# A two-block network on one core: the gates of the short layers read from the accumulator bank, one norm for both token tiles, the heads spread over other column steps

## The reference, cut to what matters

```python
for layer in range(2):
    h = _rmsnorm(x, norm_g[layer])
    parts = jnp.split(h @ w_in[layer], 8, axis=-1)
    if layer % 2 == 0:
        qa, ka, va, ga, qb, kb, vb, gb = parts
        oa = _dilated_mixture(rope(qa), rope(ka), va)
        ob = _moba(rope(qb), rope(kb), vb)
    else:
        qc, kc, vc, gc, qd, kd, vd, gd = parts
        oc = _diff_attention(rope(qc), rope(kc), vc, lam, subln_g, lambda_init)
        od = _stick_breaking(qd, kd, vd)
    y = concat([oa * silu(ga), ob * silu(gb)])     # (oc, gc), (od, gd) in the second
    x = x + y @ w_out[layer]
```

## Time and profile before

| | |
|---|---|
| three runs | 2966.28, 2959.11, 2965.33 us; median 2965.33 |
| the profiled execution | 2962.29 us, its span 2960.5 us, so 1.8 us lie around the span |
| mean granted TensorE clock | 0.983 |
| busy: PE, PEld, DVE, ACT, POOL | 96%, 79%, 54%, 47%, 8% |
| the chain that ended last | PE 82%, DVE 8%, ACT 6%, issue 1%, POOL 1%, DMA 1% |

### The profile page before, as it was taken

How to read it: one execution, slowest core, us unless ns; L and a number is a source line. 1 busy time by engine, 2 the same in 40 slices (tenths; PEclk the granted TensorE clock), 3 DMA queues, 4 the chain that set the end, 5 groups by cost and what they waited for, 6 DMA issues and landing times.

```text
span 2960.5 us, 33218 instructions
## 1 busy us (share of the span) xinstructions
PE 2841.2 (96%) x13558; PEld 2346.8 (79%) x13558; DVE 1613.4 (54%) x2004; ACT 1402.6 (47%) x2045; POOL 234.6 (8%) x209
## 2 busy tenths in 40 slices
PE   8899999999999999999999999999999999999986
PEld 6787887777888888888888877788888888877765
DVE  5664666756554554444645545655455444476655
ACT  6554345546444444344544444644444434465563
POOL 0112332300000000000100101000000000011112
PEclk9999999999999999999999999999999999999998
DMA  6654543656666666555664423666666655554422
GB/s 211 123 115 120 106 106 85 122 180 192 185 192 191 185 191 191 187 191 190 192 190 138 140 95 129 191 185 192 191 185 190 191 188 191 190 182 143 135 93 99
DMA packets 212776, 480.85 MB, mean 162 GB/s; under 512 B 15248, under 2 KB 16272, under 8 KB 211984
## 3 DMA queue, kind: packets, MB, share of 16 engines
q1 hardware_dynamic: 210272, 467.57, 54.4%
q0 software_dynamic: 2352, 11.17, 1.1%
HBM read 476.58 MB, written 2.10 MB: 162 GB/s over the span
## 4 chain that ended last, share of the span: by engine, by line
PE 82%; DVE 8%; ACT 6%; issue 1%; POOL 1%; DMA 1%; SPq 0%; DVEq 0%; ACTq 0%; POOLq 0%
PE PS L1013 17%; PE PS L1015 17%; PE PS L1014 17%; PE PS L1062 7%; PE PS L1061 7%; PE PS L1060 7%; DVE WL L1998 2%; ACT WH L1531 1%; DVE WORK L2139 1%; PE PS L1171 1%; DVE XL L1998 1%; PE PS L1270 1%; PE PS L1359 1%; PE PS L1259 1%; PE PS L1086 1%
## 5 line engine op out<-in xcount | busy, mean ns | idle before, releaser
L1998 DVE TENSOR_TENSOR WL<-RAW,WH 128x1024 fp32r<-128x1024 f32 x827 | 1028.4, 1246 | 943.3 <-ACT WH L1531 942.3
L1531 ACT ACTIVATE WH<-RAW 128x1024 fp32r<-128x1024 f32 x831 | 874.5, 1054 | 849.3 <-PE PS L1015 524.0
L1013 PE MATMUL PS<-WH,UTH 128*128 128x512 f32 x2396 | 965.5, 403 | 25.0 <-DVE WL L1998 22.4
L1015 PE MATMUL PS<-WH,UTL 128*128 128x512 f32 x2396 | 939.9, 392 | 0.0
L1014 PE MATMUL PS<-WL,UTH 128*128 128x512 f32 x2396 | 939.3, 392 | 0.0
L1013 PEld LDWEIGHTS PS<-WH,UTH 128*128 128x128 f32 x2396 | 454.0, 189 | 124.7 <-DVE WL L1998 26.3
L1015 PEld LDWEIGHTS PS<-WH,UTL 128*128 128x128 f32 x2396 | 453.2, 189 | 98.4
L1014 PEld LDWEIGHTS PS<-WL,UTH 128*128 128x128 f32 x2396 | 454.4, 190 | 89.9 <-issue 1.9
L1062 PE MATMUL PS<-WH,HTL 128*128 128x512 f32 x656 | 259.3, 395 | 0.0
L1061 PE MATMUL PS<-WL,HTH 128*128 128x512 f32 x656 | 258.8, 394 | 0.0
L1060 PE MATMUL PS<-WH,HTH 128*128 128x512 f32 x656 | 255.4, 389 | 0.0
(11 more groups left out here) (424 smaller groups left out, 2612.2 us busy)
## 6 DMA issues: line engine op xcount, KB each, us to landing
RAW<-in_ffn_w_gu SPq DMA_DIRECT2D x352, 512.0 KB, 4.2
RAW<-in_ffn_w_down SPq DMA_DIRECT2D x176, 512.0 KB, 4.4
RAW<-in_ab_w_in SPq DMA_DIRECT2D x128, 512.0 KB, 4.7
RAW<-in_nsa_w_in SPq DMA_DIRECT2D x80, 512.0 KB, 3.7
RAW<-in_w_in SPq DMA_DIRECT2D x64, 512.0 KB, 3.9
RAW<-in_ab_w_out SPq DMA_DIRECT2D x32, 512.0 KB, 4.4
RAW<-in_nsa_w_out SPq DMA_DIRECT2D x32, 512.0 KB, 3.8
RAW<-in_w_out SPq DMA_DIRECT2D x16, 512.0 KB, 3.8
```

Source lines behind the costliest of these rows:

```text
L1013: e.matmul(o, lh, wh[:, j], start=k + j == 0, stop=False)
L1015: x = e.matmul(o, ll, wh[:, j], start=False, stop=k + j == NKT - 1)
L1531: e.activation(wh, raw, ACTF.Copy).then_inc(*a_hi.inc(s))
L1998: e.tensor_tensor(wl, raw, wh.bitcast(F32), ALU.subtract).then_inc(*v_lo.inc(s))
```

## The change

Steps of the list: `plain` pauses one round more before `pl_s`; `diff` pauses 1 + 2h rounds where it paused h, and its `df_a` is split in two (`df_a`: ScalarE scales row 0, VectorE makes the small factor; `df_b`, a round later: VectorE's sum). `stick` puts `st_z` of heads 0 and 1 in one round, 2 and 3 in the next, and all four `st_l` in one round. `y2d` is one step for both token tiles; `ot 4 0` comes one round later, `ot 5 0` four rounds behind `y2d`. The list of stage 5 becomes: `feat 5 0` R34, `df_s` R35, 37, 39, 41, `df_a` R37, 39, 41, 43, `df_b` R38, 40, 42, 44, `df_t` R39, 41, 43, 45, `st_z` R40, 40, 41, 41, `st_l` R43 (all), `st_m` R44 (all), `st_a` R46, 46, 47, 47, `st_w` R47, 47, 48, 48, `gate2 5 1` R47, `y2d` R49, `ot 5 0` R53; `gate2 5 3`, `st_o` and `ot 5 2` stay in R55, R56, R57.

Operations: for chunks 1 and 3 `z2` copies only the values (128x256); the gate half stays in the bank until `gate2` takes it with one ScalarE Silu into Z2, and that Silu frees the bank. `y2` (stage 4) and the last branch move to VectorE; `st_o` multiplies by the gate as it leaves its bank. GpSimd keeps only the gain times gate of the difference branch.

```diff
-def operand(st, k, *made):
+def operand(st, k, *made, behind=None):
...
-    yield from pause(1 if k in LEFT[st][-4:] else 2)
+    yield from pause(behind or (1 if k in LEFT[st][-4:] else 2))
...
 def plain(br, par, i):
...
-    yield from pause(2 * par + i)
+    yield from pause(1 + 2 * par + i)
...
-def close(st, br, chunk, *parts):
+def close(st, chunk, *parts):
...
-    for i in range(2):
-        yield from need(*parts[i])
-        put("y2", st, br, i)
+    for i, made in enumerate(parts):
+        yield from need(*made)
+        put("y2", st, chunk // 2, i)
...
 def diff(h, i):
...
-    yield from pause(h)
+    yield from pause(1 + 2 * h)
...
+    yield
+    put("df_b", h, i)
...
 def close_diff():
-    yield from need(("z2", 5, 1, 1))
-    put("gate2", 5, 1)
+    yield from need(*[("df_o", h, i) for h in range(4) for i in range(2)])
+    put("y2d")
...
-    for i in range(2):
-        yield from need(*[("df_o", h, i) for h in range(4)])
-        put("y2d", i)
-        yield
...
 def stick(h):
...
-    yield from pause(h)
+    yield from pause(h // 2)
...
-    yield
+    yield from pause(3 - h // 2)
...
-    yield from pause(2)
+    yield from pause(2 + h // 2)
...
-      *[close(4, br, 2 * br + 1, *[[("pl_o", br, par, i) for par in range(2)] for i in range(2)])
+      *[close(4, 2 * br + 1, *[[("pl_o", br, par, i) for par in range(2)] for i in range(2)])
...
-      *[operand(4, k, *[("y2", 4, k // 2, i) for i in range(2)]) for k in (0, 2)])
+      *[operand(4, k, *[("y2", 4, k // 2, i) for i in range(2)], behind=2 - k // 2) for k in (0, 2)])
...
-      close_diff(), close(5, 1, 3, *[[("st_o", h) for h in range(4)]] * 2),
-      operand(5, 0, ("y2d", 0), ("y2d", 1)), operand(5, 2, ("y2", 5, 1, 0), ("y2", 5, 1, 1)))
+      close(5, 1), close_diff(), close(5, 3),
+      operand(5, 0, ("y2d",), behind=4), operand(5, 2, *[("st_o", h) for h in range(4)]))
...
     def gate2_of(chunk, i):
-        base = 2048 + 256 * (i + chunk - 1)
-        return Z2[:, i, 512 * chunk + 256:512 * chunk + 512], WORK[:, base:base + 256]
+        return Z2[:, i, 512 * chunk + 256:512 * chunk + 512]
...
+        elif st == 4:
+            on.wait_ge(*v_b2.of("y", st, k // 2, t))
...
-            on.wait_ge(*g_b2.of("y", st, k // 2, t))
+            on.wait_ge(*(v_b2.of("st_o", 3) if k else v_b2.of("yg")))
...
 def z2(st, part, t):
-    sink(Z2[:, t, 512 * part:512 * part + 512], st, PARTS2.index(part), t, ("z2", st, part, t))
+    c = PARTS2.index(part)
+    if part in (0, 2):
+        sink(Z2[:, t, 512 * part:512 * part + 512], st, c, t, ("z2", st, part, t))
+        return
+    on.wait_ge(*p_mm.of(col_end[st, c]))
+    e.activation(Z2[:, t, 512 * part:512 * part + 256], banks.ap("acc", st, c, t)[:, 0:256], ACTF.Copy,
+                 scale=HR[:, t:t + 1]).then_inc(*a_z.inc("z2", st, part, t))
...
 def gate2(st, chunk):
+    c = PARTS2.index(chunk)
...
-        g, ee = gate2_of(chunk, i)
-        on.wait_ge(*a_z.of("z2", st, chunk, i))
-        e.activation(ee, g, ACTF.Exp, scale=-1.0).then_inc(*a_b2.inc("gate", st, chunk, i))
+        e.activation(gate2_of(chunk, i), banks.ap("acc", st, c, i)[:, 256:512], ACTF.Silu,
+                     scale=HR[:, i:i + 1]).then_inc(*banks.empty(a_b2, "acc", st, c, i))
+        a_b2.also("gate", st, chunk, i)
...
+def df_a(h, i):
+    P, T, s, nk = diff_of(h, i)
+    on.wait_ge(*v_b2.of("df_r", h, i))
+    e.activation(P[:, 0], P[:, 0], ACTF.Copy, scale=s[:, 4:5]).then_inc(*a_b2.inc("df_0", h, i))
...
-def y2d(i):
-    rstd(4, "y2d", i)
+def y2d():
+    on.wait_ge(*a_b2.of("df_o", 3, 1))
+    e.activation(v3(ROT[:, 256:768], 2), Y2[:, :, 0:256], ACTF.Square).then_inc(*a_b2.inc("sq"))
+    rstd(8, "y2d")
...
-def st_o(h):
-    on.wait_ge(*p_b2.of("st_o", h))
-    e.activation(Y2[:, :, 256 + 64 * h:320 + 64 * h], v3(banks.ap("st_o", h)[:, 0:128], 2),
-                 ACTF.Copy).then_inc(*banks.empty(a_b2, "st_o", h))
...
-def gate2(st, chunk):
-    for i in range(2):
-        g, ee = gate2_of(chunk, i)
-        on.wait_ge(*a_b2.of("gate", st, chunk, i))
-        e.tensor_scalar(ee, ee, 1.0, None, ALU.add).then_inc(*v_b2.inc("gate1", st, chunk, i))
-        on.wait_ge(*v_b2.last())
-        e.reciprocal(ee, ee).then_inc(*v_b2.inc("gate", st, chunk, i))
+def y2(st, br, i):
+    y = Y2[:, i, 256 * br:256 * br + 256]
+    on.wait_ge(*a_b2.of("gate", st, 2 * br + 1, i))
+    on.wait_ge(*v_b2.of("pl_o", br, 1, i))
+    e.tensor_tensor(y, y, gate2_of(2 * br + 1, i), ALU.mult).then_inc(*v_b2.inc("y", st, br, i))
...
+def st_o(h):
+    c = 1536 + 256 + 64 * h
+    on.wait_ge(*a_b2.of("gate", 5, 3, 1))
+    on.wait_ge(*p_b2.of("st_o", h))
+    e.tensor_tensor(Y2[:, :, 256 + 64 * h:320 + 64 * h], v3(banks.ap("st_o", h)[:, 0:128], 2),
+                    Z2[:, :, c:c + 64], ALU.mult).then_inc(*banks.empty(v_b2, "st_o", h))
...
-    e.tensor_scalar(P[:, 0], P[:, 0], s[:, 4:5], None, ALU.mult).then_inc(*v_b2.inc("df_0", h, i))
-    on.wait_ge(*v_b2.last())
...
+def df_b(h, i):
+    P, T, s, nk = diff_of(h, i)
+    on.wait_ge(*a_b2.of("df_0", h, i))
+    on.wait_ge(*v_b2.of("df_c", h, i))
...
-def y2d(i):
-    y = v3(Y2[:, i, 0:256], 4)
-    sq = v3(ROT[:, 256 + 256 * i:512 + 256 * i], 4)
-    ss = ST2[:, 64 + 4 * i:68 + 4 * i]
-    on.wait_ge(*g_b2.of("sq", i))
-    e.tensor_reduce(ss, sq, AX, ALU.add).then_inc(*v_b2.inc("ss", i))
+def y2d():
+    y = Y2[:, :, 0:256]
+    ss = ST2[:, 64:72]
+    on.wait_ge(*a_b2.of("sq"))
+    e.tensor_reduce(ss, v3(ROT[:, 256:768], 8), AX, ALU.add).then_inc(*v_b2.inc("ss"))
...
-    rstd(ss, ss, 64, 1.0 - LAMBDA, "y2d", i)
+    rstd(ss, ss, 64, 1.0 - LAMBDA, "y2d")
...
-    e.tensor_tensor(y, y, bc(ss, 64), ALU.mult).then_inc(*v_b2.inc("yn", i))
+    for i in range(2):
+        yi = v3(Y2[:, i, 0:256], 4)
+        e.tensor_tensor(yi, yi, bc(ss[:, 4 * i:4 * i + 4], 64), ALU.mult).then_inc(*v_b2.inc("yn", i))
+    on.wait_ge(*v_b2.last())
+    on.wait_ge(*g_b2.of("gate"))
+    e.tensor_tensor(y, y, Z2[:, :, 768:1024], ALU.mult).then_inc(*v_b2.inc("yg"))
...
 def gate2(st, chunk):
-    for i in range(2):
-        g, ee = gate2_of(chunk, i)
-        on.wait_ge(*v_b2.of("gate", st, chunk, i))
-        e.tensor_tensor(ee, ee, g, ALU.mult).then_inc(*g_b2.inc("gate", st, chunk, i))
...
-def y2(st, br, i):
-    y = Y2[:, i, 256 * br:256 * br + 256]
-    on.wait_ge(*g_b2.of("gate", st, 2 * br + 1, i))
-    on.wait_ge(*(v_b2.of("pl_o", br, 1, i) if st == 4 else a_b2.of("st_o", 3)))
-    e.tensor_tensor(y, y, gate2_of(2 * br + 1, i)[1], ALU.mult).then_inc(*g_b2.inc("y", st, br, i))
...
-def y2d(i):
-    y = v3(Y2[:, i, 0:256], 4)
-    sq = v3(ROT[:, 256 + 256 * i:512 + 256 * i], 4)
-    on.wait_ge(*a_b2.of("df_o", 3, i))
-    e.tensor_tensor(sq, y, y, ALU.mult).then_inc(*g_b2.inc("sq", i))
-    on.wait_ge(*v_b2.of("yn", i))
-    e.tensor_tensor(y, y, rep(SLN, 4), ALU.mult).then_inc(*g_b2.inc("yg", i))
-    on.wait_ge(*g_b2.of("yg", i))
-    on.wait_ge(*g_b2.of("gate", 5, 1, i))
-    e.tensor_tensor(Y2[:, i, 0:256], Y2[:, i, 0:256], gate2_of(1, i)[1], ALU.mult).then_inc(*g_b2.inc("y", 5, 0, i))
+    if (st, chunk) == (5, 1):
+        for i in range(2):
+            g = v3(gate2_of(chunk, i), 4)
+            on.wait_ge(*a_b2.of("gate", st, chunk, i))
+            e.tensor_tensor(g, g, rep(SLN, 4), ALU.mult).then_inc(*g_b2.inc("gate", i))
+        g_b2.also("gate")
...
```

More of the change, by code:

```diff
@@ L1925, in df_t @@
             @step
+            def df_a(h, i):
+                P, T, s, nk = diff_of(h, i)
+                on.wait_ge(*v_b2.of("df_r", h, i))
+                e.activation(P[:, 0], P[:, 0], ACTF.Copy, scale=s[:, 4:5]).then_inc(*a_b2.inc("df_0", h, i))
+            @step
             def df_t(h, i):
@@ L1960, in st_a @@
                 e.activation(L, Zs, ACTF.Exp).then_inc(*a_b2.inc("st_x", h))
-            @step
-            def st_o(h):
-                on.wait_ge(*p_b2.of("st_o", h))
-                e.activation(Y2[:, :, 256 + 64 * h:320 + 64 * h], v3(banks.ap("st_o", h)[:, 0:128], 2),
-                             ACTF.Copy).then_inc(*banks.empty(a_b2, "st_o", h))
             @step
```

2 lines of the change are left out of this document (removed).

## The result

The changed kernel takes 2935.14 us (median of 4 runs, 2933.53 to 2935.63) where the kernel before took 2962.3 beside it. The ratio is 0.9909 [0.9897, 0.9922]. The profiled executions are 2935.07 against 2962.29, their spans 2933.3 against 2960.5: 27.2 us to account for.

What follows compares the result with a forecast made beforehand. PE, busy 96% of the span, was taken as the bound, with its idle time and slow clock to win. 1.8 + 1.7 + 3.1 + 13.7 + 1.9 + 2.8 = 25.0 us off 2962.3 gave 2937.3, stated as 2938; range 2924 to 2952.

Steps and rivals of the forecast that it cites:

- the likeliest case: Whole kernel: the forecast itself, 25.0 us gained, 2938 us; chance 0.50.
- (a): Stage 4 scores a round later: two stops of 0.9 us covered, 1.8 us gained; what moves along taken at zero.
- (c): Middle of stage 5: 12.7 us idle against 20.5, plus 5.9 of clock, 13.7 us gained; bounds 7.8 and 27.
- (b): Last operand of stage 4: Silu and VectorE product end its stop, 1.7 us net, plus 3.1 from the clock.
- (d): Last operand of stage 5: 1.9 us gained despite a 1.4 us bank wait, plus 2.8 from the clock.
- the walk: Middle of stage 5: the step list followed with estimated durations, giving stops of 2.6, 2.6, 4.0, 2.5 and 1.0 us.
- The clock wins nothing: Whole kernel: remaining stops of 1.4 to 4 us keep the clock low; gain 13 us, 2949; chance 0.22.
- The spread covers all: Middle of stage 5: preparations two slots ahead soak up the stops; total gain 38 us, 2924; chance 0.15.
- Rivals 3 and 4: Stage 5: moved df_b stops PE at every df_t; slower, 2977 (chance 0.05), or no change, 2962 (chance 0.08).
- The signs: Stages 4 and 5: no GpSimd stops before line 1077, full clock behind last operands, 1.4 us bank wait, one Ln load.
- one sign of being wrong: Windows behind the stops that remain show clock 0.5 again; the sum then lies at rival 1 or above.
- rival 1: The rival "The clock wins nothing": gain 13 us, 2949 us; chance 0.22.

Runs made afterwards that it cites:

- The undo: The whole change, but stage 4's score softmaxes back in their old round: 2935.45 us, ratio 0.99.
- The kernel with the load taken away: The whole change plus a one-number Silu behind stage 5's norm, so the Silu table loads in idle time: 2931.56 us, ratio 0.9892.
- both spreads are undone: The whole change, but stage 5's difference softmaxes in consecutive rounds and stick-breaking heads one per round: 2939.81 us; with df_b also in df_a's round, 2942.91 us.
- the one with the operations alone: All new operations in the kernel before's old order of steps, stage-4 operands included: 2942.43 us, ratio 0.9921.
- the one with the order alone: The kernel before with only the new pauses of plain, diff and stick, old operations and operand places: 2951.57 us, ratio 0.9955.
- the version with the preparation first: The whole change plus the one-number Silu, and the next slot's preparation ahead of every rope step: 2926.99 us, ratio 0.9871.

## Why the prediction was right, and which of its terms were not

The forecast was 2938 (2937.3 against the profiled execution, which gave 2935.07), by the likeliest case. Its mechanism stands, two of its terms don't, and they fell on opposite sides: stretch by stretch it was 2.2 us too high in (a), 5.2 too low in (c) and 0.8 too high in (b) and (d) together, 25.0 forecast for 27.2 measured. That the sum came out within 2.2 us is in part luck.

**(a) failed.** It took the move of the score softmaxes as two covered stops of 0.9 and "everything behind `pl_s` moves with it" at nothing. The two stops are gone, but the one for the slot behind the second rope, 1.78 before, which I had not looked at, is 2.79, and half of 3.4 us at half clock stands behind it. 1.8 - 1.0 - 1.7 = -0.9, where 1.8 was forecast; PE began stage 4's first stop 0.3 earlier, for a reason ahead of the change, so the table shows -0.4. The undo shows the exchange of stops both ways, and why: PE goes on with that slot 29.4 to 29.6 us behind the first feature transposes in every kernel that keeps the slot behind the rope, whether the scores come a round later or not, so what PE saves ahead of it, it waits there. The 1.7 of clock is not as clear. All eight kernels with the stop of 2.8 have it, but so has the undo, with 1.78.

**(b) held.** 1.9 us measured, 1.7 forecast, and 2.6 from the clock up to the features against 3.1. The 1.41 behind the operand stayed and did not bring the clock down.

**(c) was too small by 5.2 us, and only in the stops.** The two halves of its sum can be taken apart by the window: PE is busy 82.26 of 90.02, so 7.8 idle where I walked to 12.7. Busy time fell by 88.36 - 82.26 = 6.1, where 5.9 was forecast for the clock. The walk's stops against the measured: 2.6 and 1.12 at the first head's `df_b`, 2.6 and 1.94 at the first `st_z`, 4.0 and 2.04 at the third head's `df_b`, 2.5 and 1.69 at the last head's, 1.0 and 0.67 for the slot behind the norm. The places are right, the sizes were walked 1.3 to 2.3 times too large. What made the difference can be seen at the first one (ScalarE's rows, then VectorE's):

```profile
2817.24 0.50 ACT L1928 ACTIVATE WORK<-WORK,SM 128x256 f32<-128x256 f32 x1
...
2817.74 1.99 ACT L1530 ACTIVATE WH<-RAW 128x1024 fp32r<-128x1024 f32 x2
```

```profile
2819.96 0.74 DVE L2454 SCALAR_TENSOR_TENSOR WORK<-WORK,SM 128x128 f32<-128x128 f32 x2
```

Counted from the end of the feature transposes (2802.11 here, 2806.25 in the walk), the second head's exps end at 15.7 us instead of 16.5, and from there to `df_b` there are one copy and one rest as walked. PE goes on at 18.2 instead of 19.2, for the first of the two short `df_b` is enough; and PE came there at 17.1 instead of 16.7. So the chain was walked 0.9 us too long and PE 0.5 us too early, which makes the 1.4 us between 2.5 and 1.12. The other four stops I have not taken apart in this way. On the two spreads the prediction had no separate price, and the runs say that a price for each alone would have misled: their gains don't add.

The norm needed 2878.73 + 0.69 - 2874.66 = 4.8 us from the last `df_o` copy to the gate product, 5 forecast from the earlier trace rows:

```profile
2875.36 0.69 DVE L2462 TENSOR_REDUCE SM<-BIG 128x8 f32<-128x512 f32 x1 [1.77 <-ACT BIG L1951]
...
2877.93 0.76 DVE L2468 TENSOR_TENSOR BIG<-BIG,SM 128x256 f32<-128x256 f32 x2
2878.73 0.69 DVE L2471 TENSOR_TENSOR BIG<-BIG 128x512 f32<-128x512 f32 x1
```

Of the table loads of ScalarE that the prediction counts in the middle, eight became three, as it says. In both stages together 14 became 10, for stage 4 has a new one ahead of its Silu of chunk 1 (2708.21 us, L1914). The ones of the stick-breaking heads are now one for Ln (L1968) and one for the exp behind it (L1974), where the earlier trace rows had four and three.

**(d) held.** 1.7 against 1.9, and the rest of the span 2.5 against 2.8 of clock. The 1.9 had been taken with 1.2 us for the bank's wait, though the working beside it gives 1.4; with that it is 1.7. The bank's stop is 1.36, forecast 1.4, made as the prediction put it (ScalarE):

```profile
2892.33 0.84 ACT L1626 ACTIVATE BIG<-PS,SM 128x256 f32<-128x256 f32 x2 [1.60 <-PE PS L1012]
2893.19 1.28 ACT L1914 ACT_TABLE_LOAD   x1
2894.48 0.84 ACT L1914 ACTIVATE BIG<-PS,SM 128x256 f32<-128x256 f32 x2
```

The load starts 0.02 us behind the copies and the Silu 0.01 behind the load: 1.31 us from the last copy to the Silu, no drain. The Trainium skill, page ScalarE: Activation LUTs, section What ACT_TABLE_LOAD costs, adds a drain of about 1380 ns to each switch. This trace disagrees, and the measurement decides: with the page's drain the stop would have been 1.36 + 1.38 = 2.7 us (an estimate from that page's figure). The kernel with the load taken away lost the whole 1.36.

**The rivals.** "The clock wins nothing" fell: 10.8 us of busy time went. "The spread covers all" fell as well: five stops of 0.7 to 2.0 us are left, though the result lies between it and the forecast. Rivals 3 and 4 were right that `df_b` in its new place holds PE up, and wrong in the size: it releases PE late at three of the four heads, 1.12 + 2.04 + 1.69 = 4.9 us in all, and the clock is low behind one of the three. Its own round is worth about 1.5 us where both spreads are undone; in the changed kernel the round of `df_b` alone was not tried.

**The signs.** The stops before line 1077 went, the clock is 1.00 behind both last operands, the bank's wait, the one Ln load and the norm are as said. Of the stops of 2 to 4 us that were to stay at the softmax rows only one is left, 2.04. And one sign of being wrong came true: the windows behind the stops of 2.79 and 1.99 show 0.50 and 0.57. The sum did not go to rival 1 for it, because the long low windows behind the three operand stops were the larger part and did go.

## What to carry to other kernels

When a step is moved off a stop, write down what stands behind it on every queue it now delays, and look at the stops that are already there, for one of them may grow by what the moved one loses. Here it did, because the slot was late on VectorE and not on PE. The gains of two changes of order need not add, so undo them together before calling one of them useless. And a table load that would fall at a chunk's edge, where a bank is waited for, can be paid earlier by an activation of one number.

## What the runs showed of the hardware

The length of a single stop does not tell what the clock does behind it. The same stop of 1.78 us at the same instruction was followed by full clock in the kernel before and in the one with the operations alone, and by a mean of 0.59 over 3.5 us in the one with the scores moved back:

```profile
2681.16:2684.66 3.50, 3.50 (x9) 0.59 0.55 181
```

Where the stop at this instruction is the longer one, 2.75 to 2.82 us, the clock over the next 3.5 us is 0.50 to 0.57 in all eight kernels that have it.

The stop of 1.9 to 2.0 us before the features was followed by slow transposes (5.3 us) in eight of the kernels that have it, that of before among them, and by fast ones (3.65) in five, one profile each. What decides between the two was not tried. Two stops of 1.4 to 3.1 us with some 0.6 us of work between them, as the kernel before and the one with the order alone have at both last operands, had the clock low each time (0.54 to 0.61); the 1.4 that is left of the pair in the changed kernel left it at 1.00 both times.

VectorE's products of the stage-4 rope take either 0.42 or some 0.96 us for the same 128x256. In the second rope of the changed kernel five of six are long (VectorE's rows, then GpSimd's):

```profile
2675.32 0.95 DVE L2375 TENSOR_TENSOR WORK<-BIG 128x256 f32<-128x256 f32 x1
2676.31 0.42 DVE L2378 TENSOR_TENSOR BIG<-WORK 128x256 f32<-128x256 f32 x1
2676.66 0.96 DVE L2374 TENSOR_TENSOR WORK<-BIG 128x256 f32<-128x256 f32 x1
```

```profile
2675.08 0.91 POOL L2656 TENSOR_TENSOR WORK<-BIG 128x256 f32<-128x256 f32 x1
2676.42 0.92 POOL L2659 TENSOR_TENSOR BIG<-WORK 128x256 f32<-128x256 f32 x1 [0.43 <-DVE WORK L2375]
```

The long ones begin while a product of GpSimd runs, the short one in the gap between two. In the version with the preparation first, the three that begin while GpSimd is idle (2676.73, 2677.07 and 2677.51) are short. How much of that version's gain rests on them was not tried. The Trainium skill, page SBUF — State Buffer, section Who interferes with whom, says that a VectorE instruction with two SBUF inputs contends with a GpSimd instruction that reads SBUF; these rows agree, 0.96 against 0.42.
